# A sum moved from a transfer to VectorE, two places for another sum, and a new order in one pair of blocks

## The chip, the cores and the metric

The kernel runs on one core of a Trainium2 chip. The core's engines each work through a queue of their own in order and wait for each other by semaphores (counters that an instruction raises when it ends): TensorE (PE; PEld is its weight load), VectorE (DVE), ScalarE (ACT), GpSimd (POOL) and SyncE (SP). In this kernel SP issues the weight loads, POOL issues a few transfers and otherwise works little. The metric is the device time of one execution in microseconds (us), median of several; smaller is better.

## The reference, cut to what matters

The program is three transformer blocks over 512 tokens of width 1024, in fp32. The change touches only the two convolutional feed-forward layers of the second and third block:

```python
def conv_ffn(y, w_up, conv_w, conv_b, w_down):
    up = y @ w_up                              # 512 x 1024 by 1024 x (2 * 2816)
    u, v = jnp.split(up, 2, axis=-1)           # "gate" half and "up" half
    u_pad = jnp.pad(u, ((0, 0), (CONV_WIDTH - 1, 0), (0, 0)))
    c = conv_b
    for j in range(CONV_WIDTH):                # 3 taps along the tokens
        c = c + conv_w[j] * u_pad[:, j:j + S]
    return (jax.nn.gelu(c, approximate=False) * v) @ w_down
```

The first block's two feed-forward layers are the same without taps: silu(x @ w_gate) * (x @ w_up), then the down product.

## The kernel before

**Stages.** The program is a row of fourteen stages. The four big products into 2 x 2816 columns are `up1` and `up2` (first block, silu) and `up3` and `up4` (conv_ffn, evacuation kind "conv"). Each works in 22 column blocks f of 128 gate columns and 128 up columns; the 1024 x 256 weights of one block are a pair q, 1 MB, loaded by SP into one of two places of `raw` (place q % 2) as soon as VectorE has finished with the pair before in that place.

**Exact products.** A weight is split in two fp32r numbers: ScalarE rounds it (`w_hi`), VectorE subtracts (`w_lo`); the tokens are split likewise. A product is then three matmuls (lines 1273 to 1275: hi by hi, hi by lo, lo by hi).

**Plain and seven blocks.** Blocks 0 to 5 of an up stage (`PLAIN` = 6) are multiplied plainly. Blocks 6 to 21 (the "blocks of seven") halve tokens, inner dimension and the pair of columns, and take seven products of quarters where eight would be plain. `seven_pe` issues them as seven quarters of 12 matmuls with 256 columns each. Four of them take weights as they were loaded (quads 0 to 3 of the pair: gate 1, gate 2, up 1, up 2), three take sums of quads, held in `w_sum`, `w_sum_hi`, `w_sum_lo`:

- the "third" sum, up 1 + up 2, written back over up 1 in `raw`, so that it is rounded with the pair;
- `w_sum` 0, gate 1 + third, and `w_sum` 2, that plus gate 2 (VectorE, lines 2519 and 2525);
- `w_sum` 1, gate 1 + up 1 (the "fifth").

In `up1` and `up2` VectorE forms all four. In `up3` and `up4` the third sum is an accumulating transfer from `raw` to `raw` (POOL, line 2999; 256 KB), and the fifth is a copy from memory into `w_sum` 1 (line 3004) with an accumulating transfer after it (line 3006).

**Order around a block of seven.** The order is written out by hand, engine by engine. While TensorE works on block f, the others prepare block f + 1. ScalarE (`seven_act`) in order: copies the first quarter's result out of PSUM (`keep` into `prod`, line 1998), rounds the next pair (`round_pair_summed`, line 1982), copies the third quarter's result (`keep` into `up`, line 1998), rounds the sums (line 1993), applies the first conv tap (line 1964) and the gelu (line 1971). VectorE (`conv_dve`): two conv taps (2586, 2589), the sums, the products with the gelu (2548, 2550; for a plain block 2544), joins of quarters (2609, 2621, 2628), and the rests of the weights (1782) and of the sums (2530). TensorE waits in a block for the copies by ScalarE (`seven_kept`: before its 3rd, 5th and 6th quarter), for the rests of the sums (`w_sum_lo_ready`, at the same places) and before its 7th quarter for line 2621 (`fourth_ready`).

**The first pair.** Block 6 (f == PLAIN) has a branch of its own in both functions, since at that time the last plain block (5) still has its taps, its gelu and its product to do. VectorE has at that time also the split of the tokens' quarters behind it (`xq`, lines 2560 to 2578).

**The stage's opening.** In pair 1 of `up3` and `up4` TensorE computes the norm's mean squares after the products of step k = `stats_at` (line 1260, waits for `ssum_ready` from VectorE) and spreads the roots two steps later (line 1267); line 2872 copies them for VectorE, and all of its evacuations wait for that.

Of the kernel before, what the change touches and what calls it, by code (L numbers as in the profile page):

```python
# [5 lines left out]
F32 = mybir.dt.float32  # L6
# [6 lines left out]
P = 128  # L13
# [160 lines left out]
def build(nc, x_t, vecs, weights, mixer_consts, pool_tab, small_consts, pool_w, sinks, rel_bias, out_t, scratch, skew, stop=None):  # L174
# [4 lines left out]
    with ExitStack() as ctx:  # L179
# [4 lines left out]
        def at(name, shape, dt, offset):  # L184
            return nc.alloc_sbuf_tensor_at(name, shape, dt, offset=offset)
# [6 lines left out]
        def sem(name):  # L192
            return ctx.enter_context(nc.semaphore(name))
# [41 lines left out]
        x_open = at("x_open", [P, 2 * KD * T], F32R, act_at)  # L235
        act32 = at("act32", [P, KF * T], F32, act_at)
        w_sum = at("w_sum", [P, 3 * QUAD], F32, act_at + 22 * ROOM)
        w_sum_hi = at("w_sum_hi", [P, 3 * QUAD], F32R, act_at + 25 * ROOM)
        w_sum_lo = at("w_sum_lo", [P, 3 * QUAD], F32R, act_at + 28 * ROOM)
        xq = at("xq", [P, 14 * XQ], F32R, act_at + 32 * ROOM)  # L240
# [160 lines left out]
        third_landed, copy_landed, fifth_landed = sem("third_landed"), sem("copy_landed"), sem("fifth_landed")  # L401


        NEG, ROW, INV = (tiny[:, 16 * k:16 * (k + 1)] for k in range(3))
# [732 lines left out]
        def quad(t, n, count=1):  # L1137
            return t[:, n * QUAD:(n + count) * QUAD]
# [10 lines left out]
        def summed(st, f, count):  # L1149

            n, whole = seven_index(st, f), 2 * (KF - PLAIN)
            return 4 * n + count if n < whole else 4 * whole + 2 * (n - whole) + count - 2

        def seven_banks(st, f):
            b = 2 * ((st.g0 + f) % 2)
# [89 lines left out]
        def _(pe):  # L1245
# [402 lines left out]
            for st in stages:  # L1648
# [10 lines left out]
                elif st.kind == "in":  # L1659
# [1 line left out]
                    r_hi, r_lo = (mix_hi, mix_lo) if mixed else (x_source(st.x_index)[:, 0:KD * T], x_source(st.x_index)[:, KD * T:])  # L1661
                    ready = (mix_ready, KD * ("out1", "out2", "out3").index(st.name)) if mixed else (x_ready, KD * st.x_index)

                    stats_at = {"up1": 5, "up2": 2, "up3": 3, "up4": 3}[st.name]
                    halves = st.name in ("up3", "up4")

                    def body(i, u=2, st=st, r_hi=r_hi, r_lo=r_lo, ready=ready, mixed=mixed, stats_at=stats_at, halves=halves):
# [146 lines left out]
        def _(eng):  # L1814
# [152 lines left out]
            def silu(f, f0):  # L1967

                eng.wait_ge(gate_ready, f0 + 1 + f)
                wait(eng, prod_ready, f0 + f)  # L1970
                eng.activation(gated[:, :], gate[:, :], ACT.Silu if f0 < 2 * KF else ACT.Gelu).then_inc(gated_ready, 1)

            def round_pair_summed(st, f):

                n, q = seven_index(st, f), st.q0 + f
                if st.evac == "conv":
                    eng.wait_ge(third_landed, 16 * (n - 2 * (KF - PLAIN) + 1))
                else:
                    eng.wait_ge(w_summed, summed(st, f, 2))
                eng.wait_ge(pair_done, q - 1)  # L1980
                w = slice(q % 2 * PAIR, (q % 2 + 1) * PAIR)
                eng.activation(w_hi[:, w], raw[:, w], ACT.Copy).then_inc(hi_rounded, 1)

            def round_sum(st, f, c):

                n = seven_index(st, f)
                if st.evac == "conv" and c == 1:
                    eng.wait_ge(fifth_landed, 16 * (n - 2 * (KF - PLAIN) + 1))
# [4 lines left out]
                eng.activation(quad(w_sum_hi, c), quad(w_sum, c), ACT.Copy).then_inc(w_sum_hi_ready, 1)  # L1993
# [48 lines left out]
            def seven_act(st, f, f0):  # L2042
# [22 lines left out]
                wait(eng, prod_ready, f0 + f if f > PLAIN else f0)  # L2065
                keep(up[:, 0:HALF], ra, 6 * n + 3)
                if f == PLAIN and st.evac == "conv":
                    silu(f - 1, f0)
                if more:
                    round_sum(st, nxt, 0)  # L2070
                else:
                    round_act(st, 2, f0)
                keep(prod[:, HALF:T], rb, 6 * n + 4)
# [178 lines left out]
        def _(eng):  # L2252
# [274 lines left out]
            def rest_sum(st, f, c):  # L2527

                eng.wait_ge(w_sum_hi_ready, 3 * seven_index(st, f) + c + 1)
                eng.tensor_tensor(quad(w_sum_lo, c), quad(w_sum, c), quad(w_sum_hi, c).bitcast(F32), ALU.subtract)\  # L2530
                    .then_inc(w_sum_lo_ready, 1)

            def rest_act(st, f, f0):
# [58 lines left out]
            def conv_dve(st, f, f0):  # L2592
# [17 lines left out]
                rest_weights(eng, st.q0 + nxt, 0, 0)  # L2610
                if f == PLAIN:
                    gated_product(st, f - 1, f0)
                elif more:
                    rest_sum(st, nxt, 0)
                else:
# [7 lines left out]
                    for j in range(3, 5):  # L2623
                        rest_act(st, j, f0)
                if f == PLAIN:
                    rest_sum(st, nxt, 0)
                eng.wait_ge(seven_done, 6 * n + 6)
                eng.tensor_tensor(shifted[:, 2 + HALF:], rb, up[:, 0:HALF], ALU.add).then_inc(u_ready, 1)
                if more:
# [348 lines left out]
        def _(eng):  # L2978
# [14 lines left out]
            def sums_by_transfer(st, f):  # L2993

                n, q = seven_index(st, f), st.q0 + f
                j = n - 2 * (KF - PLAIN)
                own, src = raw[:, q % 2 * PAIR:(q % 2 + 1) * PAIR], weights[st.name][f]
                eng.wait_ge(raw_landed[q % 2], 16 * (q // 2 + 1))
                eng.dma_start(quad(own, 2), quad(own, 3), accum_op=ALU.add).then_inc(third_landed, 16)
                if f == PLAIN:  # L3000
                    eng.wait_ge(ssum_ready, KD * (st.stat + 1))
                else:
                    eng.wait_ge(w_sum_lo_ready, 3 * n - 1)
                eng.dma_start(quad(w_sum, 1), quad(src, 0)).then_inc(copy_landed, 16)
                eng.wait_ge(copy_landed, 16 * (j + 1))
                eng.dma_start(quad(w_sum, 1), quad(src, 2), accum_op=ALU.add).then_inc(fifth_landed, 16)

            for st in stages:
                if st.name in ("up3", "up4"):
# [146 lines left out]
```

## Time and profile before

| | |
|---|---|
| median of 3 executions | 2037.5 us (2036.06, 2037.5, 2043.79) |
| the profiled execution | 2043.45 us, of which the span of its instructions is 2041.6 us |
| TensorE busy | 2011.4 us (99%) |
| VectorE busy | 1460.0 us (72%) |
| ScalarE busy | 987.0 us (48%) |
| GpSimd busy | 244.3 us (12%) |
| mean granted TensorE clock | 0.997 of full |
| `up3`, `up4` | from about 1080 us and 1677 us of the span |

Busy times are of one execution. A matmul's row lasts longer than its turn, since matmuls overlap: in these stages the starts of neighbours with 256 columns are 0.12 us apart, which is what counts for TensorE. The same holds in part for VectorE, where an instruction of 0.69 us that waits for nothing is followed by the next after 0.60 us.

### The profile page before, as it was taken

To read this page: it belongs to the slowest core of one execution; us is meant where nothing else is said; L and a number is where in the kernel's file an instruction comes from. 1 tells how busy PE (TensorE), PEld (TensorE's weight loads), DVE (VectorE), ACT (ScalarE), POOL (GpSimd) and SP (SyncE) were. 2 spreads that over 40 slices of the span, in tenths; PEclk is the share of its full clock that TensorE was granted. 3 is DMA by queue.
4 is the path that set the end of the run, shared out by engine and by line. 5 is a ranking of instruction groups with operands and counts; after the bars stand their busy time and mean duration, and the time that the engine had idled before them with its cause. 6 is when DMAs were issued, how large, how long until landed. Compare 5 with 4: busy or idle time off the path is not lost.

```text
span 2041.6 us, 32634 instructions
## 1 busy us (share of the span) xinstructions
PE 2011.4 (99%) x12670; PEld 1761.0 (86%) x12670; DVE 1460.0 (72%) x2427; ACT 987.0 (48%) x1607; POOL 244.3 (12%) x266
## 2 busy tenths in 40 slices
PE   9999999999999999999999999999999999999998
PEld 7899988778899988988788899888877798999887
DVE  7888833786798863587778987833657878988733
ACT  5455622254445542453454655612557754555522
POOL 0000000500000000000001221100536520122001
PEclk9999999999999999999999999999999999999999
DMA  8322233312222222321322566433356624666332
GB/s 257 122 104 104 78 100 111 131 64 85 86 101 104 99 88 96 104 104 63 93 83 83 142 181 179 115 101 105 111 132 171 162 73 124 170 181 176 91 98 70
DMA packets 90142, 236.99 MB, mean 116 GB/s; under 512 B 47729, under 2 KB 51105, under 8 KB 73617
## 3 DMA queue, kind: packets, MB, share of 16 engines
q1 hardware_dynamic: 72896, 184.04, 27.6%
q0 software_dynamic: 14768, 37.49, 8.4%
q10 hardware_dynamic: 2336, 13.52, 1.9%
q8 instruction: 96, 1.57, 0.3%
q14 instruction: 46, 0.37, 0.1%
HBM read 211.86 MB, written 7.38 MB: 107 GB/s over the span
## 4 chain that ended last, share of the span: by engine, by line
PE 86%; DVE 8%; DMA 2%; ACT 1%; issue 1%; POOL 1%; SPq 0%; DVEq 0%; ACTq 0%
PE ps L1273 27%; PE ps L1275 26%; PE ps L1274 26%; DVE act L2536 1%; PE ps L511 1%; PE ps L524 1%; DMA raw<-raw 1%; PE ps L735 1%; PE ps L717 1%; DVE w_lo L1782 1%; POOL h L3039 1%; DVE w_lo L1772 1%; PE ps L702 1%; DMA w_sum<-in_w_up 0%; DMA raw<-in_w_up 0%
## 5 line engine op out<-in xcount | busy, mean ns | idle before, releaser
L1782 DVE TENSOR_TENSOR w_lo<-raw,w_hi 128x2048 fp32r<-128x2048 f32 (+3 forms) x144 | 287.8, 1999 | 156.4 <-ACT w_hi L1754 148.6
L1273 PE MATMUL ps<-act,w_hi 128*128 128x512 f32 (+1 forms) x1026 | 376.4, 367 | 4.2 <-DVE act L2536 1.9
L1275 PE MATMUL ps<-act,w_lo 128*128 128x512 f32 (+1 forms) x1026 | 371.8, 362 | 0.0
L1274 PE MATMUL ps<-act,w_hi 128*128 128x512 f32 (+1 forms) x1026 | 371.8, 362 | 0.0
L1273 PE MATMUL ps<-xq,w_hi 128*128 128x256 f32 x1024 | 290.3, 284 | 3.3 <-DVE up L2621 3.3
L1274 PE MATMUL ps<-xq,w_hi 128*128 128x256 f32 x1024 | 289.8, 283 | 0.0
L1275 PE MATMUL ps<-xq,w_lo 128*128 128x256 f32 x1024 | 289.7, 283 | 0.0
L1273 PEld LDWEIGHTS ps<-act,w_hi 128*128 128x128 f32 x1026 | 193.5, 189 | 42.6 <-issue 7.5
L1273 PE MATMUL ps<-xq,w_sum_hi 128*128 128x256 f32 x768 | 219.7, 286 | 9.1 <-ACT up L1998 7.7
L1275 PEld LDWEIGHTS ps<-act,w_lo 128*128 128x128 f32 x1026 | 193.5, 189 | 30.4
L1275 PE MATMUL ps<-xq,w_sum_lo 128*128 128x256 f32 x768 | 218.7, 285 | 0.0
L1274 PE MATMUL ps<-xq,w_sum_hi 128*128 128x256 f32 x768 | 218.6, 285 | 0.0
L1274 PEld LDWEIGHTS ps<-act,w_hi 128*128 128x128 f32 x1026 | 193.6, 189 | 28.8
L1273 PEld LDWEIGHTS ps<-xq,w_hi 128*128 128x128 f32 x1024 | 196.7, 192 | 4.3 <-DVE up L2621 3.9
L1754 ACT ACTIVATE w_hi<-raw 128x1536 fp32r<-128x1536 f32 (+3 forms) x80 | 119.1, 1489 | 164.2 <-PE ps L1275 160.0
L1274 PEld LDWEIGHTS ps<-xq,w_hi 128*128 128x128 f32 x1024 | 196.6, 192 | 0.2
L1275 PEld LDWEIGHTS ps<-xq,w_lo 128*128 128x128 f32 x1024 | 196.5, 192 | 0.0
L1993 ACT ACTIVATE w_sum_hi<-w_sum 128x512 fp32r<-128x512 f32 x192 | 119.6, 626 | 111.6 <-PE ps L1275 71.0
L1273 PE MATMUL ps<-x_split,w_hi 128*128 128x512 f32 (+1 forms) x400 | 161.4, 403 | 0.0
L1273 PEld LDWEIGHTS ps<-xq,w_sum_hi 128*128 128x128 f32 x768 | 148.8, 194 | 10.7 <-ACT up L1998 8.6
L1275 PE MATMUL ps<-x_split,w_lo 128*128 128x512 f32 (+1 forms) x400 | 153.0, 383 | 0.0
L1274 PE MATMUL ps<-x_split,w_hi 128*128 128x512 f32 (+1 forms) x400 | 152.7, 382 | 0.0
(297 smaller groups left out, 4015.2 us busy)
## 6 DMA issues: line engine op xcount, KB each, us to landing
raw<-in_w_up SPq DMA_DIRECT2D x87, 1024.0 KB, 4.8
raw<-in_w_down SPq DMA_DIRECT2D x29, 768.0 KB, 4.2
raw<-in_w_in SPq DMA_DIRECT2D x20, 1024.0 KB, 4.8
raw<-in_w_down SPq DMA_DIRECT2D x29, 640.0 KB, 3.8
w_sum<-in_w_up POOLq DMA_DIRECT2D x64, 256.0 KB, 3.8
raw<-in_w_out SPq DMA_DIRECT2D x8, 1024.0 KB, 4.8
raw<-raw POOLq DMA_DIRECT2D x32, 256.0 KB, 4.9
raw<-in_w_in ACTq DMA_DIRECT2D x8, 1024.0 KB, 4.9
```

The source lines that it names most:

```text
L511: ins = pe.matmul(score_bank(i, hh)[:, at_:at_ + w], ring[rows, qs:qs + P], ring[rows, ks:ks + w], start=True, stop=True)
L524: ins = pe.matmul(pair_bank(c)[64 * hh:64 * hh + 64, n * P:(n + 1) * P], v_tok[:, vc:vc + 64], turned_at(u)[:, hh, at_ + j * P:at_ + (j + ...
L702: ins = pe.transpose(bank(TURN_BANK + hh)[:, to:to + P], exps_at(a, u, hh)[:, at_ + j * P:at_ + (j + 1) * P], ident)
L717: ins = pe.matmul(bank(SCORE_BANK + hh)[:, to:to + w], tile_at(a, ROPED[a][1 + c])[rows, n * P:(n + 1) * P], keys[rows, lo * P:(hi + 1) * ...
L735: ins = pe.matmul(pair_bank(c)[64 * hh:64 * hh + 64, n * P:(n + 1) * P], g_vtok[a][:, vc:vc + 64], g_turned_at(a, u)[:, hh, to:to + P], st ...
L1273: pe.matmul(own, hi, rhs_hi, start=start, stop=False, skip_group_check=more)
L1274: pe.matmul(own, hi, rhs_lo, start=False, stop=False, skip_group_check=more)
L1275: return pe.matmul(own, lo, rhs_hi, start=False, stop=stop, skip_group_check=more)
L1754: eng.activation(w_hi[:, w], raw[:, w], ACT.Copy).then_inc(hi_rounded, 1)
L1772: ins = eng.tensor_tensor(w_lo[:, w], raw[:, w], w_hi[:, w].bitcast(F32), ALU.subtract)
L1782: eng.tensor_tensor(w_lo[:, w], raw[:, w], w_hi[:, w].bitcast(F32), ALU.subtract).then_inc(lo_rounded, 1)
L1993: eng.activation(quad(w_sum_hi, c), quad(w_sum, c), ACT.Copy).then_inc(w_sum_hi_ready, 1)
```

## The change

Four edits, all for `up3` and `up4` alone:

1. The third sum is formed by VectorE (as in `up1` and `up2`), line 2526 of the changed kernel; the transfer from `raw` to `raw` is gone. ScalarE's rounding of the pair now waits for VectorE (`w_summed`) and not for the transfer.
2. The fifth sum has two places, `w_sum` 1 for even blocks and `w_sum_odd` for odd ones, each with its own semaphores, and the copy for block f + 1 is issued behind the addition for block f.
3. In block 6 VectorE does line 2621 (now 2629) ahead of the pair's rests, and the product of block 5 behind the joins; ScalarE copies the fourth quarter's result (`prod`, second half) ahead of the gelu.
4. The mean squares stand one step later in the opening (`stats_at` 4 for 3).

```diff
+        w_sum_odd = at("w_sum_odd", [P, QUAD], F32, act_at + 31 * ROOM)
...
+        def sum_at(st, f, c):
+            if c == 1 and st.evac == "conv" and f % 2:
+                return w_sum_odd[:, :]
+            return quad(w_sum, c)
...
-                    stats_at = {"up1": 5, "up2": 2, "up3": 3, "up4": 3}[st.name]
+                    stats_at = {"up1": 5, "up2": 2, "up3": 4, "up4": 4}[st.name]
...
             def round_pair_summed(st, f):
                 n, q = seven_index(st, f), st.q0 + f
-                if st.evac == "conv":
-                    eng.wait_ge(third_landed, 16 * (n - 2 * (KF - PLAIN) + 1))
-                else:
-                    eng.wait_ge(w_summed, summed(st, f, 2))
+                eng.wait_ge(w_summed, summed(st, f, 2))
...
                 keep(up[:, 0:HALF], ra, 6 * n + 3)
                 if f == PLAIN and st.evac == "conv":
+                    keep(prod[:, HALF:T], rb, 6 * n + 4)
                     silu(f - 1, f0)
...
                 wait(eng, w_sum_lo_ready, 3 * n)
-                if st.evac == "conv":
-                    eng.wait_ge(third_landed, 16 * (n - 2 * (KF - PLAIN) + 1))
-                else:
-                    eng.wait_ge(raw_landed[q % 2], 16 * (q // 2 + 1))
+                eng.wait_ge(raw_landed[q % 2], 16 * (q // 2 + 1))
+                if st.evac == "silu":
                     eng.tensor_tensor(quad(w_sum, 1), g1, u1, ALU.add).then_inc(w_summed, 1)
                     eng.wait_ge(w_summed, summed(st, f, 1))
-                    eng.tensor_tensor(u1, u1, u2, ALU.add).then_inc(w_summed, 1)
-                    eng.wait_ge(w_summed, summed(st, f, 2))
+                eng.tensor_tensor(u1, u1, u2, ALU.add).then_inc(w_summed, 1)
+                eng.wait_ge(w_summed, summed(st, f, 2))
                 eng.tensor_tensor(quad(w_sum, 0), g1, u1, ALU.add).then_inc(w_summed, 1)
...
+                eng.wait_ge(copy_landed[f % 2], turn(st, f))
+                eng.dma_start(sum_at(st, f, 1), quad(src, 2), accum_op=ALU.add).then_inc(fifth_landed[f % 2], 16)
+                if f + 1 < KF:
+                    if f > PLAIN:
+                        eng.wait_ge(w_sum_lo_ready, 3 * n - 1)
+                    copy_gate(st, f + 1)
```

VectorE's queue at the first pair of `up3`, from the second tap of block 5 to the rest of `w_sum` 1 of block 7, before:

```order
L2589 SCALAR_TENSOR_TENSOR gate<-shifted,vec,gate 128x512 [waits conv_b]
L2519 TENSOR_TENSOR w_sum<-raw 128x512 [waits third_landed,w_sum_lo_ready]
L2525 TENSOR_TENSOR w_sum<-w_sum,raw 128x512 [waits w_summed]
L2609 TENSOR_TENSOR shifted<-ps,prod 128x256 [waits gate_ready,seven_done,seven_kept]
L1782 TENSOR_TENSOR w_lo<-raw,w_hi 128x2048 [waits hi_rounded]
L2544 TENSOR_TENSOR act_75<-gated,act_75 128x512 [waits evacuated,gated_ready]
L2621 TENSOR_TENSOR up<-ps,prod 128x256 [waits prod_ready,seven_done,seven_kept]
L2530 TENSOR_TENSOR w_sum_lo<-w_sum,w_sum_hi 128x512 [waits w_sum_hi_ready]
L2628 TENSOR_TENSOR shifted<-ps,up 128x256 [waits seven_done]
L2530 TENSOR_TENSOR w_sum_lo<-w_sum,w_sum_hi 128x512 [waits w_sum_hi_ready]
```

The same place of VectorE's queue after the change:

```order
L2598 SCALAR_TENSOR_TENSOR gate<-shifted,vec,gate 128x512 [waits conv_b]
L2526 TENSOR_TENSOR raw<-raw 128x512 [waits raw_landed1,w_sum_lo_ready]
L2528 TENSOR_TENSOR w_sum<-raw 128x512 [waits w_summed]
L2534 TENSOR_TENSOR w_sum<-w_sum,raw 128x512 [waits w_summed]
L2618 TENSOR_TENSOR shifted<-ps,prod 128x256 [waits gate_ready,seven_done,seven_kept]
L2629 TENSOR_TENSOR up<-ps,prod 128x256 [waits prod_ready,seven_done,seven_kept]
L1794 TENSOR_TENSOR w_lo<-raw,w_hi 128x2048 [waits hi_rounded]
L2636 TENSOR_TENSOR shifted<-ps,up 128x256 [waits seven_done]
L2539 TENSOR_TENSOR w_sum_lo<-w_sum,w_sum_hi 128x512 [waits w_sum_hi_ready]
L2553 TENSOR_TENSOR act_75<-gated,act_75 128x512 [waits evacuated,gated_ready]
L2539 TENSOR_TENSOR w_sum_lo<-w_sum_odd,w_sum_hi 128x512 [waits w_sum_hi_ready]
```

The sum over `raw` (2526) is new and stands behind both taps of block 5; the join into `up` stands ahead of the pair's rests, and the product of block 5 (2544, now 2553) behind the joins.

ScalarE's queue at the same pair, from the copy of the first quarter's result on, before:

```order
L1998 ACTIVATE prod<-ps 128x256 [waits seven_done,fourth_ready]
L1964 ACTIVATE gate<-shifted,vec 128x512 [waits u_ready,gated_ready]
L1982 ACTIVATE w_hi<-raw 128x2048 [waits pair_done,third_landed]
L1998 ACTIVATE up<-ps 128x256 [waits seven_done,prod_ready]
L1971 ACTIVATE gated<-gate 128x512 [waits prod_ready,gate_ready]
L1993 ACTIVATE w_sum_hi<-w_sum 128x512 [waits seven_done,w_summed]
L1998 ACTIVATE prod<-ps 128x256 [waits seven_done]
```

And after:

```order
L2007 ACTIVATE prod<-ps 128x256 [waits seven_done,fourth_ready]
L1976 ACTIVATE gate<-shifted,vec 128x512 [waits u_ready,gated_ready]
L1991 ACTIVATE w_hi<-raw 128x2048 [waits pair_done,w_summed]
L2007 ACTIVATE up<-ps 128x256 [waits seven_done,prod_ready]
L2007 ACTIVATE prod<-ps 128x256 [waits seven_done]
L1983 ACTIVATE gated<-gate 128x512 [waits prod_ready,gate_ready]
L2002 ACTIVATE w_sum_hi<-w_sum 128x512 [waits seven_done,w_summed]
```

The rounding of the pair keeps its place ahead of the copy into `up`; what it waits for is now `w_summed`, raised by VectorE. The second copy into `prod` went ahead of the gelu.

## Rows read from the trace of the kernel before

**Rows 1.** What TensorE waited for, whole span: us in total, times, longest us.
```profile
PE ps L1273 <- ACT up L1998: 7.7, 4, 2.8
```

**Rows 2.** Line 2628, one per block, in `up3` and in `up4`: first and last start.
```profile
L2628 DVE TENSOR_TENSOR shifted<-ps,up x16: 418/426/427, 1156.0 to 1313.9; 128x256 f32<-128x256 f32 x16
L2628 DVE TENSOR_TENSOR shifted<-ps,up x16: 420/427/427, 1752.3 to 1903.9; 128x256 f32<-128x256 f32 x16
```

**Rows 3.** DMA issues of the page: count, size, median us from issue to landing.
```profile
raw<-raw POOLq DMA_DIRECT2D x32, 256.0 KB, 4.9
```

**Rows 4.** Chain that ended last, 1255 to 1284 us: start, us, what.
```profile
1265.77 10.77 DMA raw<-raw
...
1278.38 0.38 ACT up L1998
```

**Rows 5.** Stretches: us, busy (x count) of PE, PEld, DVE, ACT, POOL; PEclk; DMA.
```profile
1278.80:1282.20 3.40, 3.40 (x16) 3.40 (x17) 3.31 (x4) 0.84 (x3) 0.40 (x1) 0.50 0.90 154
1155.90:1159.30 3.40, 3.40 (x31) 3.40 (x30) 3.02 (x6) 1.65 (x3) 0.57 (x1) 1.00 0.94 334
```

**Rows 6.** Timeline of TensorE, opening of `up3`: start, us, instruction [idle before].
```profile
1093.87 1.02 PE L1260 MATMUL ps<-small,ssum 128*128 128x1 f32 x8 [0.74 <-DVE ssum L2451]
...
1097.58 0.60 PE L1267 MATMUL ps<-small,tiny 128*128 128x128 f32 x4
```

**Rows 7.** Timeline of TensorE, block 6 of `up3`, then of `up4`.
```profile
1150.06 0.31 PE L1273 MATMUL ps<-xq,w_sum_hi 128*128 128x256 f32 x1
...
1152.33 0.39 PE L1273 MATMUL ps<-xq,w_sum_hi 128*128 128x256 f32 x1 [0.64 <-ACT prod L1998]
...
1155.59 0.38 PE L1273 MATMUL ps<-xq,w_hi 128*128 128x256 f32 x1 [1.57 <-DVE up L2621]
...
1751.88 0.38 PE L1273 MATMUL ps<-xq,w_hi 128*128 128x256 f32 x1 [1.57 <-DVE up L2621]
```

**Rows 8.** Timeline of VectorE, `up3` from block 3's product to block 6's taps.
```profile
1131.07 0.69 DVE L2544 TENSOR_TENSOR act<-gated,act 128x512 f32<-128x512 f32 x1 [0.70 <-ACT gated L1971]
...
1150.65 0.69 DVE L2519 TENSOR_TENSOR w_sum<-raw 128x512 f32<-128x512 f32 x1
...
1152.31 2.28 DVE L1782 TENSOR_TENSOR w_lo<-raw,w_hi 128x2048 fp32r<-128x2048 f32 x1
...
1157.41 0.75 DVE L2586 SCALAR_TENSOR_TENSOR gate<-shifted,vec,gate 128x512 f32<-128x512 f32 x1 [0.35 <-ACT gate L1964]
1158.20 0.75 DVE L2589 SCALAR_TENSOR_TENSOR gate<-shifted,vec,gate 128x512 f32<-128x512 f32 x1
```

**Rows 9.** Timeline of ScalarE at the first pair of `up3`.
```profile
1147.77 1.90 ACT L1982 ACTIVATE w_hi<-raw 128x2048 fp32r<-128x2048 f32 x1
...
1158.99 0.63 ACT L1971 ACTIVATE gated<-gate 128x512 f32<-128x512 f32 x1 [1.09 <-DVE gate L2589]
1159.53 0.37 ACT L1998 ACTIVATE prod<-ps 128x256 f32<-128x256 f32 x1
```

**Rows 10.** Timeline at the first pair of `up1`: VectorE, ScalarE, TensorE.
```profile
80.07 0.69 DVE L2517 TENSOR_TENSOR raw<-raw 128x512 f32<-128x512 f32 x1
...
80.79 1.91 ACT L1982 ACTIVATE w_hi<-raw 128x2048 fp32r<-128x2048 f32 x1 [3.63 <-DVE raw L2517]
82.61 0.37 ACT L1998 ACTIVATE up<-ps 128x256 f32<-128x256 f32 x1
...
83.03 0.39 PE L1273 MATMUL ps<-xq,w_sum_hi 128*128 128x256 f32 x1 [2.71 <-ACT up L1998]
```

**Rows 11.** Timeline of VectorE in an undisturbed block of `up3`.
```profile
1225.78 0.69 DVE L2530 TENSOR_TENSOR w_sum_lo<-w_sum,w_sum_hi 128x512 fp32r<-128x512 f32 x1
1226.51 0.42 DVE L2621 TENSOR_TENSOR up<-ps,prod 128x256 f32<-128x256 f32 x1
1227.90 0.43 DVE L2628 TENSOR_TENSOR shifted<-ps,up 128x256 f32<-128x256 f32 x1 [0.96 <-PE ps L1275]
```

**Rows 12.** Timeline of TensorE at the start of the same block's 7th quarter.
```profile
1227.70 0.28 PE L1273 MATMUL ps<-xq,w_hi 128*128 128x256 f32 x1
```

More of the change, by code:

```diff
@@ L400, in build @@
         fourth_ready = sem("fourth_ready")
-        third_landed, copy_landed, fifth_landed = sem("third_landed"), sem("copy_landed"), sem("fifth_landed")
+        copy_landed, fifth_landed = ([sem(f"{name}_landed{k}") for k in range(2)] for name in ("copy", "fifth"))
         NEG, ROW, INV = (tiny[:, 16 * k:16 * (k + 1)] for k in range(3))
@@ L1151, in summed, with turn @@
             n, whole = seven_index(st, f), 2 * (KF - PLAIN)
-            return 4 * n + count if n < whole else 4 * whole + 2 * (n - whole) + count - 2
+            return 4 * n + count if n < whole else 4 * whole + 3 * (n - whole) + count - 1
+        def turn(st, f):
+            before = (KF - PLAIN) // 2 * (SEVEN.index(st.name) - 2)
+            return 16 * (before + (f - PLAIN) // 2 + 1)
+        def sum_at(st, f, c):
+            if c == 1 and st.evac == "conv" and f % 2:
+                return w_sum_odd[:, :]
+            return quad(w_sum, c)
         def seven_banks(st, f):
@@ L1987, in round_sum @@
                 if st.evac == "conv" and c == 1:
-                    eng.wait_ge(fifth_landed, 16 * (n - 2 * (KF - PLAIN) + 1))
+                    eng.wait_ge(fifth_landed[f % 2], turn(st, f))
                 else:
@@ L1992, in round_sum @@
                     eng.wait_ge(seven_done, 6 * (n - 1) + (3, 5, 6)[c])
-                eng.activation(quad(w_sum_hi, c), quad(w_sum, c), ACT.Copy).then_inc(w_sum_hi_ready, 1)
+                eng.activation(quad(w_sum_hi, c), sum_at(st, f, c), ACT.Copy).then_inc(w_sum_hi_ready, 1)
             def keep(to, own, done):
@@ L2072, in seven_act @@
                     round_act(st, 2, f0)
-                keep(prod[:, HALF:T], rb, 6 * n + 4)
+                if not (f == PLAIN and st.evac == "conv"):
+                    keep(prod[:, HALF:T], rb, 6 * n + 4)
                 if st.evac == "conv" and more:
@@ L2529, in rest_sum @@
                 eng.wait_ge(w_sum_hi_ready, 3 * seven_index(st, f) + c + 1)
-                eng.tensor_tensor(quad(w_sum_lo, c), quad(w_sum, c), quad(w_sum_hi, c).bitcast(F32), ALU.subtract)\
+                eng.tensor_tensor(quad(w_sum_lo, c), sum_at(st, f, c), quad(w_sum_hi, c).bitcast(F32), ALU.subtract)\
                     .then_inc(w_sum_lo_ready, 1)
@@ L2609, in conv_dve @@
                 eng.tensor_tensor(shifted[:, 2:2 + HALF], rc, prod[:, 0:HALF], ALU.add)
[L2610 to L2613, printed above, removed]
+                if f > PLAIN:
+                    rest_weights(eng, st.q0 + nxt, 0, 0)
+                if f > PLAIN and more:
                     rest_sum(st, nxt, 0)
-                else:
+                if not more:
                     for j in range(3):
@@ L2625, in conv_dve @@
                 if f == PLAIN:
-                    rest_sum(st, nxt, 0)
+                    rest_weights(eng, st.q0 + nxt, 0, 0)
                 eng.wait_ge(seven_done, 6 * n + 6)
                 eng.tensor_tensor(shifted[:, 2 + HALF:], rb, up[:, 0:HALF], ALU.add).then_inc(u_ready, 1)
+                if f == PLAIN:
+                    rest_sum(st, nxt, 0)
+                    gated_product(st, f - 1, f0)
                 if more:
@@ L2995, in sums_by_transfer, with copy_gate @@
                 n, q = seven_index(st, f), st.q0 + f
[L2996 to L2999, printed above, removed]
+                src = weights[st.name][f]
                 if f == PLAIN:
                     eng.wait_ge(ssum_ready, KD * (st.stat + 1))
[L3002 to L3006, printed above, removed]
+                    copy_gate(st, f)
+                eng.wait_ge(copy_landed[f % 2], turn(st, f))
+                eng.dma_start(sum_at(st, f, 1), quad(src, 2), accum_op=ALU.add).then_inc(fifth_landed[f % 2], 16)
+                if f + 1 < KF:
+                    if f > PLAIN:
+                        eng.wait_ge(w_sum_lo_ready, 3 * n - 1)
+                    copy_gate(st, f + 1)
+            def copy_gate(st, f):
+                eng.dma_start(sum_at(st, f, 1), quad(weights[st.name][f], 0)).then_inc(copy_landed[f % 2], 16)
             for st in stages:
```

## The prediction, made before the changed kernel was timed

> **What bounds the kernel now.** I read the page's table of busy times first: TensorE is busy 99% of the span, so only its idle time and its stretches at the lower clock can be gained or lost. Then its waits: the one large releaser in the stages of the change is ScalarE's copy into `up`, 7.7 us in 4 waits, the longest 2.8 [rows 1]. Then the spacing of the blocks by line 2628, which runs once in each. Undisturbed, a block of seven takes TensorE 7 quarters x 12 matmuls x 0.12 us = 10.08 us, so 15 steps should take 151.2. In `up4` they take 1903.9 - 1752.3 = 151.6, in `up3` 1313.9 - 1156.0 = 157.9 [rows 2]. Some block of `up3` is therefore late, and the chain around its wait names the cause: the transfer `raw<-raw`, 4.9 us by the median [rows 3], took 10.77 there and released the copy into `up` by way of the pair's rounding [rows 4]. Last, the timelines of the opening and the first pair, where each stage loses its other idle time: 0.74 [rows 6], 0.64 and 1.57 [rows 7].
>
> The sum is made against the profiled execution, 2043.45 us. It lies 5.95 above the median, about what the late block cost it (below).
>
> **Term 1, the third sum leaves the transfers.** The stretch from the second to the last block loses what it has above 151.2: 6.7 us in `up3`, 0.4 in `up4`, together 7.1. This includes the clock: after the 2.8 us wait the granted clock was 0.50, that is the 1.2 GHz level, and 16 matmuls ran in 3.4 us where 28.4 belong [rows 5]. 2043.45 - 7.1 = 2036.35, which the two faster executions agree with (2036.06, 2037.5): an accident of the profiled one goes, and of the others little. VectorE waits for the pair's load in place of the transfer; since the pair two back frees its place about a block earlier, nothing should be late next. Bounds: -7.1, and -5 if a load is late once.
>
> The Trainium skill ("DMA: Bandwidth & Descriptors", section "Anatomy of one DMA — SWDGE (gpsimd) path") gives a transfer issued by GpSimd about 2.0 us plus bytes by 436 GB/s, which is my estimate of 2.6 us for 256 KB. By that no third sum could be late, term 1 would be nothing and the total about 2053. The 4.9 and 10.77 us contradict it, so it gets no chance.
>
> **Term 2, one more sum on VectorE in each block.** An independent sum of 512 columns is followed by the next after about 0.60 us, a dependent one after 0.73, its 0.69 plus the semaphore (1225.78 to 1226.51 shows such a step [rows 11]). In a steady block I let everything behind it move by 0.73. TensorE waits there for line 2621 before its 7th quarter. VectorE could begin that line at 1225.78 + 0.60 = 1226.38; now 1227.11; it ends 0.42 later at 1227.53, and TensorE sees it at 1227.58. Its 7th quarter started at 1227.70, without a wait [rows 12]. A margin of 0.12 us stays. So I take nothing; the cover is TensorE's own 6th quarter. If it is gone, an overrun of 0.1 in 28 steady blocks costs 2.8; more than that is a rival.
>
> **Term 3, the first pair of each stage.** This speaks against the change. ScalarE's rounding of the next pair stands ahead of its copy into `up`, for which TensorE's 5th quarter of block 6 waits. Before, it needed only the transfer and began at 1147.77 [rows 9]. Now it needs VectorE's up 1 + up 2, and VectorE reaches its sums only behind both taps of block 5: its first sum stood at 1150.65, at the end of a backlog without a pause of more than a few hundredths since 1131.07 [rows 8]. Step by step in `up3`:
>
> - VectorE's backlog starts later by the opening's edit: without the wait the mean squares would have started about 1092.97 (1093.87 less the 0.74 and the 0.16 by which matmuls overlap), a step is (1097.58 - 1093.87 - 1.02) / 2 = 1.35, and 1092.97 + 1.35 = 1094.32 is 0.45 later than before. The spread of the roots follows 3.71 behind as now, less some 0.1 for a start without a wait: 1097.93, 0.35 later [rows 6]. Block 6's own pair adds one dependent sum, 0.73. The sum for block 7 starts at 1150.65 + 0.35 + 0.73 = 1151.73 and ends at 1152.42.
> - ScalarE rounds from 1152.45, and its copy starts 1.82 later, as in `up1` (80.79 to 82.61 [rows 10]): 1154.27, done 1154.64. TensorE goes on at 1154.70.
> - It could have begun that quarter between 1149.1 and 1150.1: it did so at 1150.06 [rows 7], and 0.74 of idle time ahead of it is gone. I take 1149.8, since the tokens' rests on VectorE are late by 1.08 too and give part of it back. A new wait of 4.9 us.
> - The 5th quarter's result is there at 1156.40. VectorE does the join into `up` (0.33 to the next), the pair's rests (2.20), the next join (0.33), two rests of sums and the product of block 5 (3 x 0.60): the taps of block 6 start at 1161.10 and, with the step of 0.79 between 1157.41 and 1158.20 [rows 8], at 1161.89, and end at 1162.64. ScalarE's gelu follows (0.54 to the next instruction, as 1158.99 to 1159.53 [rows 9]), then its copy into `prod` from 1163.20 to 1163.57. TensorE's 3rd quarter of block 7 starts at 1163.6. By its own work it was due five quarters and a restart after 1154.70 (7.2 + 0.1), at 1162.0: a second wait of 1.6.
> - Before, that quarter started at 1160.00, right behind its copy (1159.53 + 0.37 [rows 9]). Stage by stage the loss is 3.6 plus 0.1 to 0.2 for the slow first matmuls after a wait (0.39 [rows 7] against 0.28 [rows 12]): 3.8. The old waits of 0.64 and 1.57 and the opening's are inside this difference, since both ends are clock readings of the same place.
>
> `up4` has the same orders and the same old wait of 1.57 at 1751.88 [rows 7]: 3.8 again. The same wait, smaller, can already be read in `up1`, where the sum is VectorE's: ScalarE waits 3.63 for it and TensorE 2.71 for the copy [rows 10]. Bounds for a stage: below, 1.6, if VectorE's steps overlap enough that the sum comes at 1150.65 as before and the second wait goes; above, 5.0, if each wait costs a few tenths more.
>
> **Term 4, the clock.** After the 2.8 us wait TensorE ran 3.4 us at 1.2 GHz, a loss of (28.4 - 16) x 0.12 = 1.5 us; after 1.57 us it stayed at 2.4 GHz, with 31 rows in the same length [rows 5]. A wait of 4.9 us is nearer the first. Part of the slow stretch hides in the second wait, which ends when VectorE and ScalarE say so: I take 1.1 a stage, between 0.3 and 1.5.
>
> **Terms at nothing.** The fifth sum by turn gives its two transfers a whole block more; they come no later than before, and if one did, ScalarE would wait 1 or 2 us once. POOL loses 32 issues. Edit 3 in ScalarE takes away the wait of 0.64, which is inside term 3.
>
> **Sum.** 2043.45 - 7.1 + 2 x 3.8 + 2 x 1.1 = 2046.15; I say 2046.2, 0.4% above the median. Half a percent, about what a measurement of this kernel can tell from no change, is 10.2 us: faster is below 2027.3, slower above 2047.7. The terms' bounds set its own range: two stages at 3.8 + 1.1 with about 1 us to either side give 2043 to 2050, a third of it above 2047.7.
>
> **Rivals.**
> - *The clock stays up* through the long wait, or the slow stretch hides in full: 2046.15 - 2.2 = 2044. Against it stand the rows of the 2.8 us wait. 5%.
> - *Faster: ScalarE is not held in the first pair.* If the load of pair 7 is early and VectorE gets to its sum before ScalarE needs it, all old waits there go: 0.64 + 1.57 + 0.74 and their restarts, 3.1 a stage, so 2036.35 - 6.2 = 2030. For it: edits 3 and 4 aim at exactly these waits. Against it: ScalarE is there at 1147.77, and no row lets VectorE's sum come before 1150.65. 7%, of which the better part below 2027.3 only if the steady blocks gain as well; I count it as faster all the same.
> - *Slower: VectorE overruns in every block.* If the added sum costs more than the margin of 0.12, TensorE waits before its 7th quarter in each of 28 steady blocks. It decides from 0.85 us for the added sum on; at 0.95 to 1.1 us the price is 28 x 0.1 to 0.25 = 2.8 to 7 on top, 2049 to 2053. For it: the margin is smaller than the error of my reading. Against it: 0.73 is measured for such a step. 10%.
> - *Nothing else moves:* that the third sum goes on by transfer cannot be; its line is gone.
>
> **How the numbers follow.** Forecast 78%, of which 21 above 2047.7; clock 5; faster 7; slower 10. So faster 7%, same 57 + 5 = 62%, slower 21 + 10 = 31%. The range from 2039 to 2051 leaves out the faster rival, the upper part of the slower one and the forecast's edges, about 2 in 10.
>
> **What will show it.** In the profile of the changed kernel: TensorE waits once in each of `up3` and `up4` for a copy into `up` for 4.5 to 5 us, and ScalarE's rounding (line 1991) ahead of it 3.5 to 4 us for VectorE's line 2526; about 7 us later a second wait of some 1.6 us for a copy into `prod`; a clock of 0.50 behind the first; line 2636 x16 over 151 to 152 us in both stages; no transfer `raw<-raw`. Term 1 is wrong if a block is late in the old manner, term 2 if TensorE waits for VectorE's line 2629 block after block, term 3 if the long waits are missing or half as long, term 4 if the clock stays at 1.00 behind them.

## The result, and the profile after

The changed kernel takes 2045.88 us (median of 6 executions, 2045.26 to 2046.55) against 2036.95 for the kernel before (6 executions, 2036.06 to 2043.79): ratio 1.0035, 95% interval 1.0019 to 1.0051 (the two medians alone give 1.0044). The forecast was 2046.2, in a range from 2039 to 2051, with 62% on a change of less than half a percent.

TensorE's waits by the page of the changed kernel, answering to [rows 1]: us in total, times, longest.

```profile
PE ps L1285 <- ACT up L2007: 12.4, 4, 4.7
...
PE ps L1285 <- ACT prod L2007: 2.3, 2, 1.3
```

Line 2636 in `up3`, then in `up4`, answering to [rows 2]: its duration, first and last start.

```profile
L2636 DVE TENSOR_TENSOR shifted<-ps,up x16: 418/427/427, 1157.7 to 1309.8; 128x256 f32<-128x256 f32 x16
L2636 DVE TENSOR_TENSOR shifted<-ps,up x16: 419/427/427, 1752.5 to 1904.9; 128x256 f32<-128x256 f32 x16
```

No block is late any more: 152.1 and 152.4 us for 15 steps (the second wait shown below lies inside both). Most of the price stands in the first pair. The timelines at the same place of `up3` as [rows 7 to 9] (start, us, instruction, idle time before it), VectorE first:

```profile
1149.49 0.69 DVE L2526 TENSOR_TENSOR raw<-raw 128x512 f32<-128x512 f32 x1
1150.22 0.69 DVE L2528 TENSOR_TENSOR w_sum<-raw 128x512 f32<-128x512 f32 x1
...
1155.16 0.42 DVE L2629 TENSOR_TENSOR up<-ps,prod 128x256 f32<-128x256 f32 x1 [3.19 <-issue]
```

ScalarE:

```profile
1150.21 1.91 ACT L1991 ACTIVATE w_hi<-raw 128x2048 fp32r<-128x2048 f32 x1 [3.50 <-DVE raw L2526]
1152.03 0.37 ACT L2007 ACTIVATE up<-ps 128x256 f32<-128x256 f32 x1
...
1161.40 0.63 ACT L1983 ACTIVATE gated<-gate 128x512 f32<-128x512 f32 x1 [1.85 <-DVE gate L2598]
1161.94 0.37 ACT L2007 ACTIVATE prod<-ps 128x256 f32<-128x256 f32 x1
```

TensorE:

```profile
1152.45 0.39 PE L1285 MATMUL ps<-xq,w_sum_hi 128*128 128x256 f32 x1 [4.67 <-ACT up L2007]
...
1162.36 0.38 PE L1285 MATMUL ps<-xq,w_sum_hi 128*128 128x256 f32 x1 [0.95 <-ACT prod L2007]
```

Read it from the bottom: TensorE waits 4.67 us for a copy that had its data all along; the copy stands in ScalarE's queue behind a rounding that waits 3.50 us for VectorE's sum; and that sum stands at the end of VectorE's backlog. While TensorE waits, VectorE in its turn has nothing to do for 3.19 us, because its next instruction (2629) needs the quarter that TensorE can't start. The second wait, 0.95, is the gelu of block 6 ahead of the copy into `prod`. The clock behind the long wait (same columns as [rows 5]):

```profile
1152.85:1156.26 3.41, 3.41 (x18) 3.41 (x18) 1.10 (x2) 1.49 (x3) 0.00 (x0) 0.50 0.00 0
```

To compare kernels without the noise of other stages, I read from each timeline the time between the first matmul behind the stage's opening wait for `x_open` (in `up3` at 1080.68 before and 1078.43 after) and the 558th after it (in block 8), for `up3` and `up4`, and from there to the first matmul of `up4` (for `filler` without its additional matmuls):

```
                     up3, first pair  up4, first pair  rest to up4   median of executions
before                     97.37            97.54         498.93      2036.95 (others below)
after                     102.13           102.43         492.38      2045.88
turn_alone                 97.59            97.33         492.34      2033.66
third_dma                  97.54            97.29         492.34      2033.84
sum_alone                 100.67           101.42         492.35      2043.54
old_pair                  101.44           101.32         492.38      2043.96
keep_first                 99.10            98.84         492.36      2038.85
sum_early                  98.73            98.71         492.35      2039.97
filler                    101.46           101.20         492.36      2044.01
double                    103.69           103.41         496.53      2056.07
order_by_transfer          96.92            96.66         492.38      2032.47
product_on_gpsimd          97.45            96.47         492.38      2035.47
```

One execution of order_by_transfer (2178.40 us, mean granted clock 0.85) and one of the kernel before beside it (4785.15 us) count as slow and are not in the ratios.

The ledger of the two profiled executions: +4.76 and +4.89 in the first pairs, -6.55 for the late block; from block 8 of `up4` to the end of that stage there is no change (130.35 and 130.45 us). The span rose by 2.7 only (2041.6 to 2044.3), for two more reasons. `up3` starts 2.25 earlier: in `up1` TensorE's wait for the same copy was 1.51 and not 2.71 [rows 10], and the 3.41 us at a clock of 0.50 behind it are missing. No edit touches `up1`, and this wait lies between 1.51 and 2.85 in the twelve profiled executions. In the other direction, the time from the last product of `up4` to the end grew by 1.74. The last store landed at 2039.50 before and at 2039.97 after; what ended last was GpSimd's closing instruction, a DRAIN. Before and after (duration in ns, start):

```profile
L179 POOLq DRAIN  x1: 6075/6075/6075, 2035.3 to 2035.3; - x1
L179 POOLq DRAIN  x1: 8001/8001/8001, 2036.1 to 2036.1; - x1
```

It lasts 6.08 us in the five profiled kernels whose third sum is a transfer and 8.00 in the seven where VectorE forms it. So edit 1 also costs 1.9 us at the very end, in none of the table's stretches. Why the drain is longer with 32 transfers fewer is open.

### The profile page after: what moved, and what is told of

The parts are those of the page before. It is cut to its first block, busy times and chain, and to the rows that moved or that the text cites. A ratio compares the mean times of both kernels' runs of the same rounds, so it can differ in the third digit from the quotient of the medians.

```text
span 2044.3 us, 32634 instructions
## 1 busy us (share of the span) xinstructions
PE 2009.6 (98%) x12670; PEld 1760.4 (86%) x12670; DVE 1479.7 (72%) x2459; ACT 987.5 (48%) x1607; POOL 216.1 (11%) x234
## 4 chain that ended last, share of the span: by engine, by line
PE 85%; DVE 10%; issue 2%; ACT 1%; POOL 1%; DMA 1%; SPq 0%; DVEq 0%; ACTq 0%; POOLq 0%
PE ps L1285 27%; PE ps L1286 26%; PE ps L1287 26%; DVE act L2545 1%; DVE w_lo L1794 1%; PE ps L512 1%; PE ps L525 1%; PE ps L736 1%; DVE xq L2587 1%; PE ps L718 1%; DVE w_lo L1784 1%; PE ps L703 1%; DVE gate L2595 1%; DMA pw<-in_pool_w 0%; DVE xq L2569 0%
## 5 line engine op out<-in xcount | busy, mean ns | idle before, releaser
L1285 PEld LDWEIGHTS ps<-xq,w_sum_hi 128*128 128x128 f32 x768 | 148.8, 194 | 17.2 <-ACT up L2007 13.2
L1286 PEld LDWEIGHTS ps<-xq,w_sum_hi 128*128 128x128 f32 x768 | 148.8, 194 | 0.0
```

Of the source, the lines that this page charges most:

```text
L1285: pe.matmul(own, hi, rhs_hi, start=start, stop=False, skip_group_check=more)
L1286: pe.matmul(own, hi, rhs_lo, start=False, stop=False, skip_group_check=more)
```

## The experiments

They ran in three groups (third_dma, sum_alone, keep_first and filler; turn_alone, old_pair, double and order_by_transfer; sum_early and product_on_gpsimd). The kernel before, beside each group, had medians of 2038.98 (31 executions, 2034.24 to 2047.04), 2038.30 and 2041.08. Ratios are to it.

**third_dma: edit 1 undone.** The transfer comes back in GpSimd's queue ahead of the fifth's addition, with a semaphore for each of the two places.

```diff
+                eng.wait_ge(raw_landed[q % 2], 16 * (q // 2 + 1))
+                eng.dma_start(quad(own, 2), quad(own, 3), accum_op=ALU.add).then_inc(third_landed[f % 2], 16)
...
-                eng.tensor_tensor(u1, u1, u2, ALU.add).then_inc(w_summed, 1)
```

> The changed kernel with edit 1 alone undone: the third sum (up 1 + up 2) is an accumulating transfer again, edits 2 to 4 stay. Theory D (the first pair of a stage is bound by VectorE's backlog; edit 1 adds the sum to it and ScalarE's rounding ahead of the copy into up turns that into a long wait): no wait over 2 us on the copy into up in up3 and up4, clock up throughout them, and no gain from edits 2 to 4 either, since the backlog of the tokens' rests ends when it did: 2036.5, between 2035 and 2038. Rival S (only ScalarE's place in its queue matters, so without edit 1 the old waits of 0.64, 1.57 and 0.74 go): about 2030. Rival O (the loss comes from edits 2 to 4): 2045 to 2046.

2033.84 (2033.21 to 2034.51), ratio 0.9973 (0.9962 to 0.9985). Theory D's mechanism held: the first pairs take what they took before (97.54 and 97.29 against 97.37 and 97.54), so edits 2 to 4 gain nothing there. The time is 1.2 below its range, for a reason that it didn't contain: no block is late and the executions hardly scatter. The changed kernel's median is 12.0 above this one, of which 4.6 and 5.1 stand in the first pairs and 1.9 in the drain: edit 1 carries the loss.

**turn_alone: the kernel before with edit 2.**

```diff
+                eng.wait_ge(copy_landed[f % 2], turn(st, f))
+                eng.dma_start(sum_at(st, f, 1), quad(src, 2), accum_op=ALU.add).then_inc(fifth_landed[f % 2], 16)
+                if f + 1 < KF:
+                    if f > PLAIN:
+                        eng.wait_ge(w_sum_lo_ready, 3 * n - 1)
+                    copy_gate(st, f + 1)
```

> The kernel before with edit 2 alone: the fifth sum has two places by turn, so that GpSimd's queue waits for a copy long landed; the third sum stays a transfer, the first pair and the opening are as before. Theory Q (the third sum was late because it stood in GpSimd's queue behind the wait for the copy into the one place and right behind the fifth's addition): third sums of 3.3 us by the median as in third_dma, no late block, 2033.5 in a narrow spread, between 2032.5 and 2035.5. Rival L (the transfer raw to raw is late by itself, and third_dma owed its time to edits 3 and 4): late blocks stay, a median near 2039 and a spread of several us.

2033.66 (2033.45 to 2035.24), ratio 0.9981 (0.9971 to 0.9991). Theory Q held. GpSimd's queue in `up3` of the kernel before (start, us to issue, idle before it):

```profile
1259.46 0.57 POOL L3004 DMA_DIRECT2D w_sum<-in_w_up  x1 [4.05 <-DVE w_sum_lo L2530]
1265.23 0.87 POOL L3006 DMA_DIRECT2D w_sum<-in_w_up  x1 [5.20 <-DMA w_sum<-in_w_up]
1265.77 1.22 POOL L2999 DMA_DIRECT2D raw<-raw  x1
```

and of turn_alone:

```profile
1224.85 0.57 POOL L3023 DMA_DIRECT2D w_sum<-in_w_up  x1 [5.13 <-DVE w_sum_lo L2543]
1226.74 0.86 POOL L3011 DMA_DIRECT2D raw<-raw  x1 [1.33 <-DMA raw<-in_w_up]
1227.95 0.87 POOL L3016 DMA_DIRECT2D w_sum<-in_w_up  x1 [0.35 <-DMA w_sum<-in_w_up]
```

Before, the third sum was issued behind a wait for another transfer (the copy, 5.20 us here) and 0.54 us behind the fifth's addition. By turn, its own load releases it, and the addition comes 1.2 us after it: its median falls from 4.9 to 3.3 us.

```profile
raw<-raw POOLq DMA_DIRECT2D x32, 256.0 KB, 3.3
```

The wait ahead of the third sum and the addition right ahead of it went together, and no run separates them. In the late block of the kernel before, the third sum was issued 1.44 us after its own load had landed and then took 10.77, 5.9 more than the median: the larger part of the delay was in the transfer itself. ScalarE's rounding waited for it:

```profile
1276.56 1.91 ACT L1982 ACTIVATE w_hi<-raw 128x2048 fp32r<-128x2048 f32 x1 [3.75 <-DMA raw<-raw]
```

**sum_alone: the kernel before with edit 1.**

```diff
-                eng.dma_start(quad(own, 2), quad(own, 3), accum_op=ALU.add).then_inc(third_landed, 16)
...
+                eng.tensor_tensor(u1, u1, u2, ALU.add).then_inc(w_summed, 1)
+                eng.wait_ge(w_summed, summed(st, f, 2))
```

> The kernel before with edit 1 alone: VectorE forms the third sum, and the fifth sum's place, the order of the first pair and the opening are as before. Theory D: a wait on the copy into up of about 4 us in the first pair of up3 and of up4, with the low clock behind it, but no second wait, since VectorE does the pair's rests and the product of block 5 during it: 1.8 plus 1.1 for the clock in each stage, 2036.4 + 5.8 = 2042, between 2040.5 and 2043.5. Rival: edit 1 carries the whole loss, 2045 to 2046. Rival: edit 1 costs nothing and the loss is edit 3's order, 2036 to 2037.

2043.54 (2042.80 to 2044.60), ratio 1.0020 (1.0008 to 1.0033), just above theory D's range: +3.30 and +3.88 in the first pairs, with one wait each. The rest of `up3` takes 492.35, so edit 1 by itself ends the late block too.

```profile
1151.48 0.39 PE L1273 MATMUL ps<-xq,w_sum_hi 128*128 128x256 f32 x1 [4.09 <-ACT up L1995]
```

In `up4` the clock was low for 6.80 us, 5.77 of them with TensorE busy, one reason why this run cost more than I expected; the drain of 8.00 us is in its time as well:

```profile
1743.20:1750.00 6.80, 5.77 (x27) 5.77 (x28) 4.71 (x7) 2.93 (x6) 0.00 (x0) 0.50 0.42 134
```

**old_pair: edit 3 undone in the changed kernel.**

```diff
-                if f > PLAIN:
-                    rest_weights(eng, st.q0 + nxt, 0, 0)
+                rest_weights(eng, st.q0 + nxt, 0, 0)
+                if f == PLAIN:
+                    gated_product(st, f - 1, f0)
```

> The changed kernel with edit 3 alone undone: ScalarE and VectorE go through the first pair in the old order, all else as changed. Theory D: the wait of 4.7 us on the copy into up stays, the second wait, for the copy into prod, goes, since VectorE does the pair's rests and the product of block 5 while TensorE waits: 1.5 a stage less, 2045.9 - 3.1 = 2042.8, or up to 1.5 more where the low clock lasts as long as in sum_alone (6.8 us in up4): 2042.5 to 2044.5. Rival (edit 3 costs nothing, the second wait only moves): 2045.5 to 2046.3.

2043.96 (2042.65 to 2045.82), ratio 1.0023 (1.0012 to 1.0035). The long wait stays at 4.67, the second is gone. Edit 3 costs 0.69 and 1.11 us in the two stages (102.13 - 101.44, 102.43 - 101.32), less than the 1.5 expected: the second wait that it adds is 0.95 and 1.32, and the clock was at 0.50 for longer behind the long wait here, 4.23 and 4.60 us.

**keep_first: the copies ahead of the rounding.**

```diff
-                if more:
+                if more and not (f == PLAIN and st.evac == "conv"):
                     round_pair_summed(st, nxt)
...
                     silu(f - 1, f0)
+                    round_pair_summed(st, nxt)
```

> The changed kernel, with ScalarE's rounding of the next pair in block 6 of up3 and up4 put behind the copies into up and prod and the gelu, so that the copies no longer wait for VectorE's sum. Theory D: the wait of 4.7 us goes and the clock stays up, but VectorE's backlog holds TensorE elsewhere (before the 7th quarter by 1.5 to 2 us, for the pair's rests by 0.7, for the copy into prod by 1.6): 1.7 a stage, 2036.4 + 3.4 = 2039.8, between 2038.5 and 2041.5. Rival S (ScalarE's order is the whole cause): 2036.5 or, if the old waits go as well, about 2030.

2038.85 (2038.45 to 2039.50), ratio 0.9998 (0.9989 to 1.0008): theory D. Of edit 1's loss in the first pairs 1.56 and 1.55 us are left (against third_dma). The wait of 4.67 us has turned into three, for VectorE twice and for ScalarE behind VectorE's taps:

```profile
1151.99 0.38 PE L1285 MATMUL ps<-xq,w_hi 128*128 128x256 f32 x1 [1.69 <-DVE up L2630]
1154.29 0.36 PE L1285 MATMUL ps<-xq,w_hi 128*128 128x256 f32 x1 [0.60 <-DVE w_lo L1794]
1158.72 0.39 PE L1285 MATMUL ps<-xq,w_sum_hi 128*128 128x256 f32 x1 [1.32 <-ACT prod L2007]
```

**sum_early: VectorE's sum moved ahead of block 5.** The function holds the sum alone; `sum_pair` leaves it out for block 7.

```diff
                     rest_sum(st, PLAIN, 1)
+                    if conv:
+                        third_sum(st, PLAIN + 1)
```

> The changed kernel with one instruction moved: in up3 and up4 VectorE forms the third sum of block 7 at the end of plain block 4, ahead of the evacuations of block 5, so that it is there some 4 us before ScalarE wants to round the pair; ScalarE's order is as changed. Theory D (VectorE's whole backlog binds the first pair under edit 1, its order only says where TensorE waits): the wait of 4.7 us shrinks to 2, shorter waits come behind it, and the time is that of keep_first, 2038.9, between 2038 and 2040. Rival S (ScalarE's wait for the sum is the whole cause): no wait is left of edit 1, 2034 to 2036.

2039.97 (2038.82 to 2041.50), ratio 0.9992 (0.9980 to 1.0005). By the stretches it equals keep_first within 0.4 us (98.73, 98.71). ScalarE doesn't wait for the sum any more but for block 5's evacuation, which now stands behind the sum in VectorE's queue, and TensorE waits for the copy into `up` as before, though for less:

```profile
1147.43 0.81 ACT L1976 ACTIVATE gate<-shifted,vec 128x512 f32<-128x512 f32 x1 [3.22 <-DVE shifted L2721]
1150.37 0.38 PE L1285 MATMUL ps<-xq,w_sum_hi 128*128 128x256 f32 x1 [1.65 <-ACT up L2007]
```

TensorE still loses 1.36 and 1.17 us against before, 1.19 and 1.42 against third_dma.

**filler: TensorE kept at work during the long wait.** The 30 products go to a bank that is not read.

```diff
+                    for k in range(30):
+                        pe.matmul(spare, of_pair(8)[k % 4][0], xq[:, XQ:XQ + HALF], start=True, stop=True)
```

> The changed kernel with 30 matmuls of 256 columns into a bank that nothing reads, ahead of the long wait in block 6 of up3 and up4: they fill about 3.6 of the 4.7 us. Theory: the granted clock then stays at 1.00 behind the wait and each stage gets back what the low clock cost, 1.0 us: 2045.9 - 2.0 = 2043.9, between 2043 and 2044.7. Rival (the second wait, for the copy into prod, takes in the slow stretch whole): 2045.9, unchanged. Rival (nothing of the slow stretch is hidden): 1.7 a stage, 2042.5.

2044.01 (2043.01 to 2044.44), ratio 1.0024 (1.0014 to 1.0035). Behind the wait the clock stays up, and 28 matmuls run where 18 did:

```profile
1152.40:1155.80 3.40, 3.40 (x28) 3.40 (x29) 1.62 (x2) 1.88 (x4) 0.00 (x0) 1.00 0.03 5
```

The 36 matmuls from the long wait to the end of block 6 take 4.56 us here in both stages; in the changed kernel they took 5.91 and 5.84. By the stretches 0.67 us came back in `up3` and 1.23 in `up4`: in `up3` the second wait grew from 0.95 to 1.33, and the long wait ended 0.26 later after the stretch's first matmul than in the changed kernel.

**double: one more sum on VectorE in each steady block.** (There are 28 such blocks, not 30 as the expectation says.)

```diff
+                    first = quad(w_sum, 2)
+                    eng.tensor_tensor(first, quad(own, 0), quad(own, 2), ALU.add).then_inc(twice, 1)
```

> The changed kernel with one more dependent sum on VectorE in each of 30 blocks (w_sum 2 as gate 1 + third, then + gate 2, in two instructions): 0.73 us a block. Theory (the change left a margin of 0.1 to 0.2 us before the 7th quarter, and VectorE is full over a block): TensorE waits for line 2629 in every block, 0.25 us by the mean, 4.1 a stage: 2045.9 + 8.2 = 2054, between 2051 and 2058. Rival (there is still a margin of 0.7 or more): 2046 to 2046.5. Rival (no margin was left at all): 30 x 0.73 = 22, 2068.

2056.07 (2055.68 to 2056.75), ratio 1.0089 (1.0071 to 1.0107): 10.2 more than the changed kernel. The rest of `up3` grows by 4.15 us, in waits like this one (28 of them in the two stages):

```profile
1189.12 0.39 PE L1286 MATMUL ps<-xq,w_hi 128*128 128x256 f32 x1 [0.18 <-DVE up L2636]
```

So the first additional sum fitted, and a second does not.

**order_by_transfer: third_dma in another order.** In block 6 ScalarE rounds the pair ahead of the tap (word by word: copy, rounding, copy into `up`, tap, copy, gelu); in block 7:

```diff
+                    for step in "aRutpg":
+                        first_pair_act(st, step, n, ra, rb, f0)
...
+                late = st.evac == "conv" and f == PLAIN + 1
+                if st.evac == "conv" and f > PLAIN and not late:
                     silu(f - 1, f0)
                 keep(prod[:, 0:HALF], ra, 6 * n + 1)
+                if late:
+                    silu(f - 1, f0)
```

> third_dma (third sum by transfer, edits 2 to 4) with another order: in block 6 ScalarE copies into up and prod and applies the gelu ahead of rounding the next pair's w_sum and behind rounding the pair itself, which goes ahead of the tap; in block 7 its copy into prod goes ahead of block 6's gelu. Theory D (VectorE's backlog binds the first pair whatever the order on ScalarE): the waits move to other places and 0.6 a stage is gained, 2033.8 - 1.2 = 2032.6, between 2031.5 and 2034. Rival S (ScalarE's order binds): 3 us a stage, 2028.

2032.47, ratio 0.9971 (0.9960 to 0.9981), the fastest version here, 1.2 below turn_alone in the same group. As theory D has it, the first pairs gain 0.6 us each over third_dma and not 3.

**product_on_gpsimd: the same, with one product moved off VectorE.**

```diff
+                    eng.tensor_tensor(own_act(PLAIN - 1), gated[:, :], own_act(PLAIN - 1), ALU.mult).then_inc(prod_ready, 1)
```

> order_by_transfer with the product of block 5 (one instruction of 512 columns, 0.60 us of VectorE) done by GpSimd in up3 and up4. Theory D (VectorE's backlog binds the first pair): the backlog is 0.6 shorter in each stage, 2032.5 - 1.2 = 2031.3, between 2030.5 and 2032.2. Rival (GpSimd's product comes too late for the gelu of block 6, or slows VectorE): 2032.5 or more.

2035.47 (2034.20 to 2040.71), ratio 0.9974 (0.9960 to 0.9989), in the group whose kernel before was at 2041.08. By the stretches nothing is gained: 97.45 and 96.47 against 96.92 and 96.66. GpSimd took 1.71 us, and VectorE's subtraction beside it took 2.70 in place of 2.28:

```profile
1150.54 1.71 POOL L3099 TENSOR_TENSOR act<-gated,act 128x512 f32<-128x512 f32 x1 [4.27 <-ACT gated L1984]
```

```profile
1151.70 2.70 DVE L1795 TENSOR_TENSOR w_lo<-raw,w_hi 128x2048 fp32r<-128x2048 f32 x1
```

So 0.42 of the 0.60 saved was given back, as the rival has it, and theory D's 1.2 us stay unproven by this run. The Trainium skill ("SBUF — State Buffer", section "SBUF: two separate sides") says that VectorE, when both its inputs are in SBUF, and a GpSimd instruction that reads SBUF share a pair of ports that one of them holds for a whole instruction. The trace agrees in kind: GpSimd ended at 1152.25, 0.55 us after VectorE's start, and VectorE lost 0.42.

## Why the prediction was right, and where it was not

- **The total is right in part by luck.** On the profiled executions a change of +2.7 was forecast and +2.7 came (2043.45 to 2046.11). Of it 9.65 stand in the first pairs (2 x 4.9 forecast) and -6.55 in the late block (-7.1 forecast). Two items that the prediction doesn't have nearly cancel: -2.25 before `up3`, from one execution to the next, and +1.74 at the end, with the longer drain.
- **Term 1** held for `up3` (6.7 forecast, 6.55 measured), and sum_alone shows that edit 1 does it; the 0.4 for `up4` didn't come. What the prediction missed is that edit 2 by itself does it as well, with the transfer kept (turn_alone), for 9.9 us less than edit 1 by itself. It put the fifth sum by turn at nothing, "they come no later than before": I looked at the fifth sum's own transfers and not at what is queued behind their wait on GpSimd. Beside edit 1 that zero is right (492.38 against 492.35 in sum_alone).
- **"An accident of the profiled one goes, and of the others little"** is wrong for the kernel before in general: its 31 executions beside the first experiments spread over 12.8 us, with a median 5 above those of turn_alone and third_dma. That the spread is late third sums is inferred and not shown: turn_alone and third_dma spread over less than 2, but product_on_gpsimd, whose slowest third sum took 6.70 in the profiled execution, over 6.5. And 2036.35 is no kernel without late sums; those two are at 2033.7. The 5.95 that was put down to the late block is near it by chance, since the profiled execution also had the slow start of `up3`.
- **Term 2** held. In a steady block of the changed kernel VectorE's line 2629 starts at 1228.20 and ends at 1228.62, and TensorE never waits for it:

```profile
1228.20 0.42 DVE L2629 TENSOR_TENSOR up<-ps,prod 128x256 f32<-128x256 f32 x1
1229.00 0.43 DVE L2636 TENSOR_TENSOR shifted<-ps,up 128x256 f32<-128x256 f32 x1 [0.38 <-PE ps L1287]
```

  VectorE's idle time before the join fell from 0.96 [rows 11] to 0.38. (The step from 1225.78 to 1226.51, which the prediction reads as a dependent one, is not: line 2621 doesn't read that sum. The 0.73 holds all the same, 1149.49 to 1150.22 above.) And double shows how near the edge this is: the slower rival (an overrun in every block) is what one more sum brings, not this one.
- **Term 3** held in each link: the sum for block 7 starts 1.09 later than before, counted from where the stretch of `up3` starts (1.08 forecast), rounding's wait 3.50 (3.5 to 4), copy 1.82 behind it, TensorE's wait 4.67 (4.9), second wait 0.95 and 1.32 (1.6). The sum of terms 3 and 4 was put at 4.9 a stage and is 4.76 and 4.89.
- **Term 4** was 1.1 a stage; filler gives 0.67 and 1.23, and the clock fell as forecast.
- **What the prediction did not see** is what lies under term 3. It named ScalarE's place in its queue; keep_first and sum_early take that wait away, each in another manner, and both keep 1.2 to 1.7 us a stage. This fits VectorE's whole backlog of the first pair, which edit 1 lengthens by two dependent sums (0.73 each, 1.5 together); product_on_gpsimd, which was to shorten that backlog, couldn't confirm it. The order on ScalarE decides the remaining 3 us: whether both engines stand still for each other, and whether the clock falls. The prediction didn't see the drain at the end either.
- **The faster rival** (2030, old waits gone) is answered by third_dma: even with ScalarE free, edits 3 and 4 move the old waits and end none.

## What to carry to other kernels

When a transfer is late, look first at what its issuing queue waited for: a second place for another sum took a wait and an addition from ahead of the late transfer, and gained more than moving the late sum to a compute engine. Before an operation is put on an engine that is 72% busy over the span, ask how full it is in the stage: here VectorE was idle for 1.4 us in 10.08 in a steady block, 0.96 of them ahead of the join, and had nothing left in the first pair. And a new producer of something that stands at the head of an in-order queue delays all that is behind it, even what has its data.

## What the runs showed of the hardware that was not expected

The granted clock fell to 0.50 behind waits of like length for differing times: 3.41 us behind one of 4.67 us in the changed kernel, 6.80 us around one of about 4 us in `up4` of sum_alone, and not at all in filler, where matmuls cut the wait to 1.07. Part of such a stretch can lie inside the wait itself, as the 5.77 us of 6.80 show. What decides its length is left open. An accumulating transfer within `raw` of 256 KB took 3.3 us by the median when its own load released it, and 4.9, once 10.77, when it followed another accumulation by 0.54 us. GpSimd's closing DRAIN lasted 6.08 us in the five kernels in which GpSimd issues 122 transfers and 8.00 in the seven in which it issues 90; the cause is open.
